# A decoder layer on one core: weight blocks rounded and subtracted whole, and the products of the feed-forward units accumulated in another order

## The chip, the cores and the metric

The kernel runs on one core of one Trainium2 chip. The metric is the device time of one execution in microseconds. The median of three executions of the kernel before is 1142.85 us (1142.00 to 1143.32).

## What is computed

One decoder layer on x of 512 tokens by 1024 features, all in float32: a feed-forward half-step, a mixer (attention in several forms), a second feed-forward half-step and a last norm.

```python
x = x + 0.5 * swiglu(rmsnorm(x, norm_ffn1), ffn1_w_in, ffn1_w_out)
x = x + hybrid_mixer(rmsnorm(x, norm_mix), ...)     # compressed, selected, windowed and dilated attention, gates
x = x + 0.5 * swiglu(rmsnorm(x, norm_ffn2), ffn2_w_in, ffn2_w_out)
return rmsnorm(x, norm_final)

def swiglu(h, w_in, w_out):            # w_in 1024 x 5632, w_out 2816 x 1024
    u, v = jnp.split(h @ w_in, 2, axis=-1)
    return (jax.nn.silu(u) * v) @ w_out
```

## The kernel before

**Three passes.** Each float32 product is made of three matmuls on rounded parts: hi x hi, hi x lo, lo x hi. ScalarE writes the rounded part of a weight block (`w_hi`, an ACTIVATE), VectorE subtracts it from the block (`w_lo`, a TENSOR_TENSOR), and TensorE needs both. Two slots of `w_hi` and `w_lo` alternate, so ScalarE can round the block of step g only when TensorE has finished step g - 2.

**The feed-forward block** is a list of segments (`SEGMENTS`): P (the narrow first block, features in 256 columns, straight products), U1, D0, U2, U3, D1, U4, U5, D2. A U segment makes 512 columns of both halves of w_in. It does this by a scheme of seven products of half-size blocks instead of eight: seven steps, each with its own combination of activation blocks (`A11`, the sums `S1` to `S4`, ...) and of weight blocks (`OPERAND`), and the results are combined into gate and value. One step is 2 x 12 matmuls of 128x512, first for token group g = 0, then g = 1. The weight combinations (`dve_diff`, `dve_t1`, `dve_t2`, `dve_t4`) are VectorE instructions of 128x2048 in the raw buffers. The gated products of one U unit are turned by TensorE (`pe_turn`, two halves) and split again into `pu_hi`, `pu_lo` (`act_turned`, `dve_turned`); the PSUM banks 6 and 7 hold both halves in turn, so half 1 is turned only after the `pu_lo` of half 0. A D segment multiplies two turned units with w_out, in four steps, and adds into `x_nat`. The whole block runs twice, i = 0 before the mixer and i = 1 behind it.

**Order.** Every engine's instructions are written out by hand in a fixed order; the semaphores in `up_sems` count what is done. For U units it stands in `act_unit`, `dve_unit` and `pe_unit`, for P in `act_plain`, `dve_plain`, `pe_plain`. `pe_bank_free` says which read of a bank TensorE waits for. In the attention part `pe_attend` goes by pairs of `ITEMS`: it transposes the probabilities of items n and n + 1, fills in a piece of projection (`pe_fill`), makes the scores of n + 2 and n + 3, then the value products of n and n + 1. Item 5 is the compressed attention; its scores are 128 very small matmuls (two records each in the trace).

**Head.** SyncE's queue brings four weight pairs of the P block (`load_pair`) and x (`load_x`) by turns, a weight pair first.

Of the kernel before, what the change touches and what calls it, by code (L numbers as in the profile page):

```python
# [26 lines left out]
ALU = mybir.AluOpType  # L27
# [7 lines left out]
P = 128  # L35
T = 512
# [65 lines left out]
def build(nc, x, positions, norm_ffn1, ffn1_w_in, ffn1_w_out, norm_mix, w_in, cmp_pos, cmp_w1, cmp_w2,  # L102
# [3 lines left out]
    with outer:  # L106
# [51 lines left out]
        A11, S3, A12, S1, S4, S2, A22 = range(7)  # L158
        SUMS = (S3, S1, S4, S2)
# [138 lines left out]
        B11, B12, B21, B22, B_DIFF, B_MINUS = range(6)  # L298

        def raw_of(u, b):  # L300
            return raws[{B11: 2, B12: 3, B22: 1, B21: 0, B_DIFF: 4, B_MINUS: 2}[b]]

        OPERAND = (B11, B_DIFF, B21, B12, B22, B_MINUS, B21)
        D_RAW = (3, 1, 2, 4)

        def op_raw(g):

            kind, n, g0 = [seg for seg in SEGMENTS if seg[2] <= g][-1]
            if kind == "P":
                return raws[4 - g]  # L310
            if kind == "U":
                return raw_of(n, OPERAND[g - g0])
            return raws[D_RAW[g - g0]][:, 0:ktiles_of(2 * n + (g - g0) % 2) * T]

        RAW_COUNT, raw_at = [0] * 5, {}
        for kind, n, g0 in SEGMENTS[1:]:
            for b, r in ((B11, 2), (B12, 3), (B22, 1), (B21, 0)) if kind == "U" else enumerate(D_RAW):
# [5 lines left out]
        for j in range(N_UNITS):  # L323
# [42 lines left out]
                   "plain": 1 + TT, "silu_plain": TT, "minus": 5, "diff": 5, "t1_ready": 5, "t2_ready": 5, "t4_ready": 5,  # L366
                   "op_hi": 2 * OPS, "op_lo": 2 * OPS, "product": 70, "down": 48, "chain_copied": 30, "v11": 10, "w7": 10,
                   "w5": 10, "e1": 10, "u12": 10, "y": 10, "v21": 10, "silu12": 10, "silu22": 10, "prod1": 12, "prod2": 12,
# [234 lines left out]
        def up_bank(kind, g, u):  # L603
            return ps[:, {"chain": 0, "first": 2, "second": 4}[kind] + g, 0:cols_of(u)]
# [28 lines left out]
        def op_landed(eng, i, g, half):  # L633
# [10 lines left out]
            elif o in (0, 2, 4):  # L644
                r, value = raw_at[kind, n, OPERAND[o]]
                eng.wait_ge(raw_landed[r], value + i * RAW_COUNT[r])
            else:
                eng.wait_ge(*up(i, {1: "diff", 3: "t1_ready", 5: "t2_ready", 6: "t4_ready"}[o], n))
# [45 lines left out]

        def load_up(sp, i, u, b, wi):
# [12 lines left out]
        def load_down(sp, i, d, o, wd):  # L708
# [3 lines left out]
            sp.dma_start(raws[D_RAW[o]][:, 0:nk * T].rearrange("p (k c) -> p k c", k=nk),  # L712
                         ktiles(wd[0])[:, k0:k0 + nk, half * T:half * T + T]).then_inc(raw_landed[D_RAW[o]], 16)

        def sync_up(sp, i, wi, wd):

            for kind, n, g in SEGMENTS[2:]:
                if kind == "D":
                    u, g0 = 2 * n + 1, first_op("U", 2 * n + 1)
                    sp.wait_ge(*up(i, "op_lo", 2 * (g0 + 4)))  # L720
                    load_down(sp, i, n, 0, wd)
                    sp.wait_ge(*up(i, "op_lo", 2 * (g0 + 5)))
                    load_down(sp, i, n, 1, wd)
                    sp.wait_ge(*up(i, "t2_ready", u))
                    load_down(sp, i, n, 3, wd)
                    sp.wait_ge(*up(i, "op_lo", 2 * (g0 + 6)))
                    sp.wait_ge(*up(i, "t4_ready", u))
                    load_down(sp, i, n, 2, wd)
                elif before_unit(n)[0] == "U":
                    g0 = first_op("U", n - 1)  # L730
                    sp.wait_ge(*up(i, "op_lo", 2 * (g0 + 4)))
                    load_up(sp, i, n, B12, wi)
                    sp.wait_ge(*up(i, "op_lo", 2 * (g0 + 5)))
                    load_up(sp, i, n, B22, wi)
                    sp.wait_ge(*up(i, "op_lo", 2 * (g0 + 6)))
                    sp.wait_ge(*up(i, "t4_ready", n - 1))
                    load_up(sp, i, n, B11, wi)
                    sp.wait_ge(*up(i, "op_lo", 2 * (g0 + 7)))
                    load_up(sp, i, n, B21, wi)
                else:  # L740
# [3 lines left out]
                    sp.wait_ge(*up(i, "op_lo", 2 * (gd + 1)))  # L744
                    load_up(sp, i, n, B12, wi)
                    sp.wait_ge(*up(i, "op_lo", 2 * (gd + 2)))
                    load_up(sp, i, n, B22, wi)
                    sp.wait_ge(*up(i, "op_lo", 2 * (gd + 3)))
                    load_up(sp, i, n, B11, wi)
# [9 lines left out]
        def _(sp):  # L759
            xv = x[0].rearrange("(t p) d -> p t d", p=P)  # L760

            def load_x(part, m0, m1, n):
                for tt in range(0, TT, n):
# [1626 lines left out]
```

## Time and profile before

| | |
|---|---|
| median of 3 runs | 1142.85 us |
| the profiled execution, its own time | 1144.03 us |
| its span, first to last instruction | 1142.2 us |
| TensorE busy | 1123.4 us, 98% |
| VectorE, ScalarE busy | 788.8 us, 517.7 us |

TensorE works nearly without a hole. Its matmuls overlap, so one of 128x512 has a duration of 0.39 us in the records but the next one starts 0.227 us later; a step of a U unit takes 24 of these, 5.44 us. In the timelines below a row gives the start, the time, the engine, the line, the operation and, in brackets, the idle time before it with what ended it.

### The profile page before, as it was taken

Reading aid. Unit: us, or ns where it says so; the run is one execution under the profiler, and the core shown is the slowest. Engines: PE = TensorE matmul, PEld = TensorE weight load, DVE = VectorE, ACT = ScalarE, POOL = GpSimd, SP = SyncE. Lnnn points to the kernel's source line nnn. Section 1 sums busy time; section 2 is a strip of 40 time slices with the busy share of each in tenths; the row PEclk is TensorE's granted clock in tenths of the full one; section 3 lists DMA queues with packets and bytes.
Section 4 is the critical chain, followed back from the end, with each engine's and each line's share of the span. In section 5 each row is a group of like instructions: output and inputs, shape, how many; then the busy total and the mean of one; then the engine's idle time right before and its main releaser. Section 6 shows DMA issues by size and latency. Waiting matters only on the chain.

```text
span 1142.2 us, 16722 instructions
## 1 busy us (share of the span) xinstructions
PE 1123.4 (98%) x6799; PEld 925.1 (81%) x6799; DVE 788.8 (69%) x1110; ACT 517.7 (45%) x757; POOL 137.0 (12%) x174
## 2 busy tenths in 40 slices
PE   8999999999999999999999999999999999999997
PEld 6778888888888987877778888888887888888885
DVE  7985888679955466566676344555795789459845
ACT  6642564245534233443445523356742565146533
POOL 1000000000010472346771000000000000000000
PEclk9999999999999999999999999999999999999999
DMA  8051326113514631413132232522052226204401
GB/s 305 24 203 37 111 74 221 37 43 106 184 47 122 153 84 43 96 54 82 45 83 50 75 101 80 181 90 101 10 184 74 74 74 221 74 8 141 147 1 74
DMA packets 111548, 111.78 MB, mean 98 GB/s; under 512 B 30896, under 2 KB 76384, under 8 KB 111472
## 3 DMA queue, kind: packets, MB, share of 16 engines
q1 hardware_dynamic: 106912, 104.97, 29.0%
q0 software_dynamic: 4400, 5.61, 1.8%
q8 instruction: 54, 0.88, 0.3%
q14 instruction: 22, 0.18, 0.1%
q10 hardware_dynamic: 160, 0.14, 0.0%
HBM read 105.71 MB, written 2.10 MB: 94 GB/s over the span
## 4 chain that ended last, share of the span: by engine, by line
PE 90%; DVE 7%; ACT 1%; issue 1%; DMA 0%; SPq 0%; DVEq 0%; ACTq 0%
PE ps L1994 11%; PE ps L1996 11%; PE ps L1995 11%; PE ps L1844 9%; PE ps L1845 8%; PE ps L1846 8%; PE ps L2010 6%; PE ps L2011 6%; PE ps L2012 6%; PE ps L1912 2%; PE ps L2128 2%; PE ps L2172 1%; PE ps L2201 1%; DVE w_lo L1500 1%; DVE probs L1458 1%
## 5 line engine op out<-in xcount | busy, mean ns | idle before, releaser
L1500 DVE TENSOR_TENSOR w_lo<-raw,w_hi 128x1024 fp32r<-128x1024 f32 (+1 forms) x124 | 142.0, 1185 | 65.0 <-ACT w_hi L1007 64.9
L1007 ACT ACTIVATE w_hi<-raw 128x1024 fp32r<-128x1024 f32 (+1 forms) x124 | 121.0, 1024 | 115.3 <-PE ps L2012 108.2
L2010 PE MATMUL ps<-w_hi,pu_hi 128*128 128x512 f32 x352 | 138.3, 393 | 0.1
L2012 PE MATMUL ps<-w_hi,pu_lo 128*128 128x512 f32 x352 | 137.1, 389 | 0.0
L2011 PE MATMUL ps<-w_lo,pu_hi 128*128 128x512 f32 x352 | 137.1, 389 | 0.0
L1994 PE MATMUL ps<-w_hi,xg_hi 128*128 128x512 f32 x320 | 125.3, 392 | 1.5 <-DVE square L1604 1.5
L1995 PE MATMUL ps<-w_lo,xg_hi 128*128 128x512 f32 x320 | 124.6, 389 | 0.0
L1996 PE MATMUL ps<-w_hi,xg_lo 128*128 128x512 f32 x320 | 124.5, 389 | 0.0
L1270 DVE TENSOR_TENSOR w_lo<-w_raw,w_hi 128x1024 fp32r<-128x1024 f32 (+4 forms) x42 | 75.3, 1793 | 54.6 <-ACT w_hi L890 54.6
L1844 PE MATMUL ps<-xg_hi,w_hi 128*128 128x512 f32 x272 | 108.5, 399 | 0.0
L1846 PE MATMUL ps<-xg_hi,w_lo 128*128 128x512 f32 x272 | 106.1, 390 | 0.0
L1845 PE MATMUL ps<-xg_lo,w_hi 128*128 128x512 f32 x272 | 106.0, 390 | 0.0
L1007 ACT ACTIVATE w_hi<-w_raw 128x1024 fp32r<-128x1024 f32 x72 | 72.2, 1052 | 66.3 <-PE ps L1996 66.3
L890 ACT ACTIVATE w_hi<-w_raw 128x2048 fp32r<-128x2048 f32 (+2 forms) x30 | 55.8, 1861 | 88.7 <-PE ps L1846 76.2
L1994 PE MATMUL ps<-w_hi,sum_hi 128*128 128x512 f32 x240 | 93.9, 391 | 0.0
L1996 PE MATMUL ps<-w_hi,sum_lo 128*128 128x512 f32 x240 | 93.4, 389 | 0.0
L1995 PE MATMUL ps<-w_lo,sum_hi 128*128 128x512 f32 x240 | 93.4, 389 | 0.0
L1500 DVE TENSOR_TENSOR w_lo<-w_raw,w_hi 128x1024 fp32r<-128x1024 f32 x72 | 84.6, 1216 | 5.0 <-ACT w_hi L1007 5.0
L2010 PEld LDWEIGHTS ps<-w_hi,pu_hi 128*128 128x128 f32 x352 | 66.1, 188 | 14.1 <-DVE pu_lo L1561 0.9
L2012 PEld LDWEIGHTS ps<-w_hi,pu_lo 128*128 128x128 f32 x352 | 66.1, 188 | 13.7
L2011 PEld LDWEIGHTS ps<-w_lo,pu_hi 128*128 128x128 f32 x352 | 66.1, 188 | 13.3
L1994 PEld LDWEIGHTS ps<-w_hi,xg_hi 128*128 128x128 f32 x320 | 60.1, 188 | 14.7 <-DVE square L1604 2.4
(287 smaller groups left out, 2155.9 us busy)
## 6 DMA issues: line engine op xcount, KB each, us to landing
raw<-in_ffn_w_in SPq DMA_DIRECT2D x20, 1024.0 KB, 4.9
w_raw<-in_ffn_w_in SPq DMA_DIRECT2D x20, 1024.0 KB, 5.0
w_raw<-in_w_in SPq DMA_DIRECT2D x32, 512.0 KB, 4.3
raw<-in_ffn_w_out SPq DMA_DIRECT2D x14, 1024.0 KB, 5.9
w_raw<-in_ffn_w_out SPq DMA_DIRECT2D x6, 1024.0 KB, 4.9
w_raw<-in_w_in SPq DMA_DIRECT2D x24, 256.0 KB, 3.9
raw<-in_ffn_w_in SPq DMA_DIRECT2D x16, 256.0 KB, 5.7
w_raw<-in_w_out SPq DMA_DIRECT2D x8, 512.0 KB, 4.4
```

Source lines behind the costliest of these rows:

```text
L1007: nc.scalar.activation(w_hi[:, (BASE[i] + g) % 2, part], op_raw(g)[:, part], ACT.Copy).then_inc(up_sems["op_hi"], 1)
L1270: lo = V.tensor_tensor(w_lo[:, s, c], w_raw[:, s, c], w_hi[:, s, c].bitcast(F32), ALU.subtract)
L1500: V.tensor_tensor(w_lo[:, sl, part], op_raw(g)[:, part], w_hi[:, sl, part].bitcast(F32), ALU.subtract).then_inc(up_sems["op_lo"], 1)
L1844: mm(out, ah, bh, start=(first and i == 0), stop=False)
L1845: mm(out, ah, bl, start=False, stop=False)
L1846: last = mm(out, al, bh, start=False, stop=(final and i == len(pairs) - 1))
L1994: mm(bank, ah, wh, start=(k == 0 and not goes_on), stop=False, skip_group_check=goes_on)
L1995: mm(bank, ah, wl, start=False, stop=False, skip_group_check=goes_on)
L1996: last = mm(bank, al, wh, start=False, stop=(k == 3), skip_group_check=goes_on)
L2010: mm(bank, ph, wh, start=(k == 0 and start), stop=False)
L2011: mm(bank, ph, wl, start=False, stop=False)
L2012: last = mm(bank, pl, wh, start=False, stop=(stop and k == nk - 1))
```

## The change

- `act_op` and `dve_op` round and subtract the weight block of every step from the third on (g >= 2) in one instruction of 128x2048 each; before, in two of 128x1024. TensorE's wait for the first half of a block is so a wait for all of it.
- The seven steps of a U unit come in another order, with three pairs of banks ("x", "z", "y"): steps 3, 4 and 5 go on accumulating in bank x on top of what is there, step 6 in bank y. VectorE's fourteen combinations of a unit become six (`dve_v11`, `dve_c22`, `dve_v21`), ScalarE's negated copy (`act_minus`) is gone. Step 5 now waits for `dve_c22`, which reads bank x after step 4.
- U1 has an order of its own (`dve_first_unit`); the P unit's two halves are turned after steps 1 and 3 of U1, before after steps 0 and 1.
- In the first P block, one sum, the difference for U1 and the copy of the other gains come later on VectorE.
- In the attention, the scores of item 5 are made in two portions around the value products of item 2, and the filled-in projection comes before the transposes of item 5.
- The first portion of x is loaded ahead of the first weight pair. The loads of later blocks follow the new release order of the raw buffers.

```diff
@@ OPERAND, raw buffers of the down steps
-        OPERAND = (B11, B_DIFF, B21, B12, B22, B_MINUS, B21)
-        D_RAW = (3, 1, 2, 4)
+        OPERAND = (B11, B_DIFF, B21, B_T2, B12, B22, B21)
+        D_RAW = ((4, 2, 3, 1), (4, 2, 3, 1), (4, 2, 3, 4))
@@ block.sync
+            load_x(sp, 0, 0, 2, 2)
             load_pair(sp, 0, 0, ffn1_w_in)
-            load_x(0, 0, 2, 2)
             load_pair(sp, 0, 1, ffn1_w_in)
@@ act_op (dve_op alike)
-            for half in range(2):
-                act_op_half(act, i, g, half)
+            if g < 2:
+                for half in range(2):
+                    act_op_half(act, i, g, half)
+                return
+            op_landed(act, i, g, 0)
+            op_slot_free(act, i, g)
+            w = op_raw(g).shape[1]
+            nc.scalar.activation(w_hi[:, (BASE[i] + g) % 2, 0:w], op_raw(g), ACT.Copy).then_inc(up_sems["op_hi"], 2)
@@ new: the combination that step 5 waits for
+        def dve_c22(dve, i, u, g):
+            n = u - 1
+            dve.wait_ge(*up(i, "product", 14 * n + 8 + g + 1))
+            dve.wait_ge(*up(i, "chain_copied", 6 * n + 2 + g + 1))
+            V.tensor_tensor(lane(u, g, 1), up_bank("x", g, u), lane(u, g, 1), ALU.add).then_inc(up_sems["c22"], 1)
@@ pe_bank_free
+            elif o == 5:
+                pe.wait_ge(*up(i, "c22", 2 * n + g + 1))
             else:
-                pe.wait_ge(*up(i, "v11", 2 * n + g + 1))
+                pe.wait_ge(*up(i, "chain_copied", 6 * n + {3: 0, 4: 4, 6: 2}[o] + g + 1))
@@ dve_plain
             if i == 0:
                 dve_rstd(dve, 0)
-                dve_more_gains(dve)
-            dve_diff(dve, i, 1)
+                dve_sum(dve, i, S4)
+            else:
+                dve_diff(dve, i, 1)
...
+                if i == 0 and tt == 1:
+                    dve_diff(dve, i, 1)
@@ pe_unit
-                if u % 2 and o < 2:
+                if u > 1 and u % 2 and o < 2:
                     pe_turn(pe, i, u - 1, o)
+                elif u == 1 and o in (1, 3):
+                    pe_turn(pe, i, 0, o // 2)
@@ pe_attend
                 pe_transpose_probs(pe, n)
+                first = n + 1 < b and ITEMS[n + 1][0] == "cmp"
+                if first:
+                    pe_fill(pe, n)
                 if n + 1 < b:
                     pe_transpose_probs(pe, n + 1)
...
                 for nn in (n, n + 1):
                     if nn < b - 1:
                         pe_values(pe, nn)
+                    if nn == n and n + 3 < b and ITEMS[n + 3][0] == "cmp":
+                        pe_scores(pe, n + 3, 1)
```

VectorE in U1 of the second feed-forward block (i = 1), from the two scalings of the P unit on. Before, where `pu_lo` is the split of the turned P unit, `raw<-raw,raw` a weight combination and `w_lo<-w_raw` the subtraction of a step:

```order
L1604 SCALAR_TENSOR_TENSOR scratch<-ps,rstd_col,scratch 128x256 [waits up_silu_plain] x2
L1500 TENSOR_TENSOR w_lo<-raw_87,w_hi 128x1024 [waits up_op_hi] x2
L1524 TENSOR_TENSOR raw_86<-raw_86,raw_85 128x2048 [waits up_diff,up_minus]
L1500 TENSOR_TENSOR w_lo<-w_raw,w_hi 128x1024 [waits up_op_hi] x2
L1561 TENSOR_TENSOR pu_lo_82<-ps,pu_hi_80 128x2x128 [waits up_p_hi] x2
L1500 TENSOR_TENSOR w_lo<-raw_86,w_hi 128x1024 [waits up_op_hi] x2
L1529 TENSOR_TENSOR raw_85<-raw_85,raw_87 128x2048 [waits up_t1_ready]
```

and now, the same stretch:

```order
L1641 SCALAR_TENSOR_TENSOR scratch<-ps,rstd_col,scratch 128x256 [waits up_silu_plain] x2
L1524 TENSOR_TENSOR w_lo<-raw_87,w_hi 128x2048 [waits up_op_hi]
L1524 TENSOR_TENSOR w_lo<-w_raw,w_hi 128x2048 [waits up_op_hi]
L1544 TENSOR_TENSOR raw_85<-raw_87,raw_85 128x2048 [waits up_op_lo,up_diff]
L1524 TENSOR_TENSOR w_lo<-raw_85,w_hi 128x2048 [waits up_op_hi]
L1549 TENSOR_TENSOR raw_86<-raw_85,w_raw 128x2048 [waits up_t2_ready]
L1524 TENSOR_TENSOR w_lo<-raw_86,w_hi 128x2048 [waits up_op_hi]
L1598 TENSOR_TENSOR pu_lo_82<-ps,pu_hi_80 128x2x128 [waits up_p_hi] x2
L1524 TENSOR_TENSOR w_lo<-w_raw,w_hi 128x2048 [waits up_op_hi]
L1571 TENSOR_TENSOR tmp_b<-ps,tmp_b 128x512 [waits up_chain_copied,up_product]
L1598 TENSOR_TENSOR pu_lo_82<-ps,pu_hi_80 128x2x128 [waits up_p_hi] x2
L1556 TENSOR_TENSOR w_raw<-w_raw,raw_85 128x2048 [waits up_op_lo,up_t1_ready,up_t2_ready]
```

The split of the first turned half moved from behind the subtraction of step 2 to behind that of step 4; each combination now reads the one before it, and the last one (`w_raw<-w_raw,raw_85`, the block of step 6) stands behind the subtraction of step 5. After it come the second `dve_c22` (L1571 on `scratch`), two `dve_v11` and the subtraction of step 6.

VectorE in U2, from its third combination on, where the L1571 rows are `dve_c22`. Now:

```order
L1524 TENSOR_TENSOR w_lo<-raw_86,w_hi 128x2048 [waits up_op_hi]
L1556 TENSOR_TENSOR w_raw<-w_raw,raw_85 128x2048 [waits up_op_lo,up_t1_ready,up_t2_ready]
L1524 TENSOR_TENSOR w_lo<-w_raw,w_hi 128x2048 [waits up_op_hi]
L1571 TENSOR_TENSOR tmp_b<-ps,tmp_b 128x512 [waits up_chain_copied,up_product]
L1571 TENSOR_TENSOR scratch<-ps,scratch 128x512 [waits up_chain_copied,up_product]
```

Here the two `dve_c22` stand behind the whole subtraction of step 5 itself; before, nothing of VectorE behind that subtraction was awaited by step 5.

TensorE around the scores of item 5, where `k_cmp` marks them, `probs` the transposes and `v_nsa` the value products (the fills of 24 matmuls in between are left out). Before:

```order
L2114 MATMUL ps<-k_cmp,pool 32x32 x128
L2201 MATMUL ps<-probs_t,v_nsa 64x128 x12
...
L2172 MATMUL ps<-const,probs 128x128 x8
L2159 MATMUL ps<-const,probs 128x128 x8
...
L2128 MATMUL ps<-pool 32x512 x8
```

and now:

```order
L2168 MATMUL ps<-k_cmp,pool 32x32 x64
L2256 MATMUL ps<-probs_t,v_nsa 64x128 x6
L2168 MATMUL ps<-k_cmp,pool 32x32 x64
L2256 MATMUL ps<-probs_t,v_nsa 64x128 x6
...
L2227 MATMUL ps<-const,probs 128x128 x8
...
L2214 MATMUL ps<-const,probs 128x128 x8
L2183 MATMUL ps<-pool 32x512 x8
```

A fill stands now between the transposes of item 4 (L2227) and of item 5 (L2214).

## Rows read from the trace of the kernel before

**Rows 1.** The page, busy time of TensorE's matmuls.
```profile
PE 1123.4 (98%) x6799; PEld 925.1 (81%) x6799; DVE 788.8 (69%) x1110; ACT 517.7 (45%) x757; POOL 137.0 (12%) x174
```
**Rows 2.** What TensorE waited for: us in total, times, longest.
```profile
PE ps L2114 <- issue: 2.4, 1, 2.4
PE ps L2159 <- DVE probs L1446: 1.9, 1, 1.9
...
PE ps L1912 <- DVE pu_lo L1561: 1.3, 2, 0.6
```
**Rows 3.** Timeline of the first feed-forward block, from P to U1.
```profile
32.39 0.39 PE L1964 MATMUL ps<-w_hi,xg_lo 128*128 128x512 f32 x1
...
32.91 2.28 DVE L1518 TENSOR_TENSOR raw<-raw,w_raw 128x2048 f32<-128x2048 f32 x1
33.50 0.47 ACT L1086 ACTIVATE scratch<-ps,rstd_col 128x256 f32<-128x256 f32 x1
35.10 0.87 DVE L1604 SCALAR_TENSOR_TENSOR square<-ps,rstd_col,square 128x256 f32<-128x256 f32 x2
35.64 0.50 PE L1994 MATMUL ps<-w_hi,xg_hi 128*128 128x512 f32 x1 [1.50 <-DVE square L1604]
```
**Rows 4.** Groups by form: busy us, mean ns of one.
```profile
L1500 DVE TENSOR_TENSOR w_lo<-raw,w_hi 128x1024 fp32r<-128x1024 f32 x116 | 136.8, 1219 | 63.4 <-ACT w_hi L1007 63.4
L1518 DVE TENSOR_TENSOR raw<-raw,w_raw 128x2048 f32<-128x2048 f32 x10 | 22.9, 2286 | 0.4
L1635 DVE TENSOR_TENSOR square<-ps,tmp_a 128x512 f32<-128x512 f32 x10 | 6.8, 679 | 0.0
L1561 DVE TENSOR_TENSOR pu_lo<-ps,pu_hi 128x256 fp32r<-128x256 f32 x8 | 3.0, 414 | 0.0
L890 ACT ACTIVATE w_hi<-w_raw 128x2048 fp32r<-128x2048 f32 x25 | 47.8, 1914 | 81.0 <-PE ps L1846 73.9 <-PE ps L2012 7.1
```
**Rows 5.** Timeline of U2, around its steps 4 and 5.
```profile
133.45 2.00 ACT L1007 ACTIVATE w_hi<-raw 128x1024 fp32r<-128x1024 f32 x2
...
138.19 0.39 PE L1994 MATMUL ps<-w_hi,sum_hi 128*128 128x512 f32 x1
```
**Rows 6.** Timeline at the start of D0.
```profile
75.48 2.01 ACT L1007 ACTIVATE w_hi<-w_raw 128x1024 fp32r<-128x1024 f32 x2 [2.54 <-PE ps L1996]
...
80.18 1.28 DVE L1561 TENSOR_TENSOR pu_lo<-ps,pu_hi 128x512 fp32r<-128x512 f32 x2
...
81.01 0.63 PE L1912 MATMUL ps<-const,tmp_b 128*128 128x128 f32 x4 [0.65 <-DVE pu_lo L1561]
```
**Rows 7.** Timeline of the second feed-forward block, P and U1.
```profile
802.98 2.00 ACT L1007 ACTIVATE w_hi<-raw 128x1024 fp32r<-128x1024 f32 x2
...
812.74 0.50 PE L1994 MATMUL ps<-w_hi,xg_hi 128*128 128x512 f32 x1
...
819.01 2.00 ACT L1007 ACTIVATE w_hi<-w_raw 128x1024 fp32r<-128x1024 f32 x2
```
**Rows 8.** Timeline of the head.
```profile
4.85 1.06 ACT L1007 ACTIVATE w_hi<-raw 128x1024 fp32r<-128x1024 f32 x1 [1.58 <-DMA raw<-in_ffn_w_in]
...
7.47 1.10 PE L1890 MATMUL ps<-const,x_nat 128*128 128x128 f32 x8 [1.08 <-DMA x_nat<-in_x]
...
8.97 0.50 PE L1968 MATMUL ps<-w_hi,xg_hi 128*128 128x512 f32 x1 [0.41 <-ACT xg_hi L895]
```
**Rows 9.** Timeline of TensorE at items 4 and 5.
```profile
455.51 1.04 PE L2172 MATMUL ps<-const,probs 128*128 128x128 f32 x8
458.45 1.16 PE L2159 MATMUL ps<-const,probs 128*128 128x128 f32 x8 [1.90 <-DVE probs L1446]
...
463.84 1.79 PE L2128 MATMUL ps<-pool 64*32 64x512 f32 x48
```
**Rows 10.** Windows: length, busy, granted clock, DMA share, GB/s.
```profile
460.00:461.00 1.00, 1.00 (x7) 0.50 0.19 64
```
**Rows 11.** The page, loads: count, KB each, us to landing.
```profile
raw<-in_ffn_w_in SPq DMA_DIRECT2D x20, 1024.0 KB, 4.9
```

More of the change, by code:

```diff
@@ L603, in up_bank @@
         def up_bank(kind, g, u):
-            return ps[:, {"chain": 0, "first": 2, "second": 4}[kind] + g, 0:cols_of(u)]
+            return ps[:, {"x": 0, "z": 2, "y": 4}[kind] + g, 0:cols_of(u)]
         def prod_lane(u, half, g):
@@ L1096, in act_unit @@
             act_op(act, i, g0 + 2)
-            if prev is not None:
+            if u > 1 and prev is not None:
                 for g in range(2):
@@ L1102, in act_unit @@
             act_op(act, i, g0 + 3)
-            if prev is not None:
+            if u > 1 and prev is not None:
                 for g in range(2):
@@ L1503, in dve_op @@
         def dve_op(dve, i, g):
-            for half in range(2):
-                dve_op_half(dve, i, g, half)
+            if g < 2:
+                for half in range(2):
+                    dve_op_half(dve, i, g, half)
+                return
+            sl, w = (BASE[i] + g) % 2, op_raw(g).shape[1]
+            dve.wait_ge(*up(i, "op_hi", 2 * g + 2))
+            V.tensor_tensor(w_lo[:, sl, 0:w], op_raw(g), w_hi[:, sl, 0:w].bitcast(F32),
+                            ALU.subtract).then_inc(up_sems["op_lo"], 2)
         def dve_diff(dve, i, u):
@@ L1586, in dve_plain @@
                 dve_op(dve, i, 1)
-            for o in (S1, S2, S4):
+            for o in (S1, S2, S4) if i else (S1, S2):
                 dve_sum(dve, i, o)
@@ L1613, in dve_unit @@
                 dve_v21(dve, i, prev, 1)
+            if u == 1:
+                dve_first_unit(dve, i, g0)
+                return
             dve_op(dve, i, g0 + 1)
-            if u == 1 and i == 0:
-                for o in SUMS[1:]:
-                    dve_sum_lo(dve, i, o)
             if prev:
@@ L1653, in dve_unit, with dve_first_unit @@
                 dve_diff(dve, i, u + 1)
[L1654 to L1660 removed]
+                dve_op(dve, i, g0 + 7)
             dve_prod1(dve, i, u, 0)
             dve_prod1(dve, i, u, 1)
+            if u % 2:
+                dve_op(dve, i, g0 + 7)
+        def dve_first_unit(dve, i, g0):
+            dve_op(dve, i, g0 + 1)
+            if i == 0:
+                dve_sum_lo(dve, i, S2)
+            dve_op(dve, i, g0 + 2)
+            dve_t2(dve, i, 1)
+            if i == 0:
+                dve_sum_lo(dve, i, S1)
+            dve_op(dve, i, g0 + 3)
+            dve_t1(dve, i, 1)
+            if i == 0:
+                dve_sum_lo(dve, i, S4)
+            dve_op(dve, i, g0 + 4)
+            for g in range(2):
+                dve_turned(dve, i, 0, 0, g)
+            dve_op(dve, i, g0 + 5)
+            dve_c22(dve, i, 1, 0)
+            for g in range(2):
+                dve_turned(dve, i, 0, 1, g)
+            dve_t4(dve, i, 1)
+            dve_c22(dve, i, 1, 1)
+            for g in range(2):
+                dve_v11(dve, i, 1, g)
+            dve_op(dve, i, g0 + 6)
+            dve_prod1(dve, i, 1, 0)
+            dve_prod1(dve, i, 1, 1)
+            dve_op(dve, i, g0 + 7)
         def dve_add(dve, i, d, half, tt):
@@ L1986, in pe_unit @@
                     pe_bank_free(pe, i, u, o, g)
-                    bank = up_bank("first" if o in (2, 6) else "second" if o == 4 else "chain", g, u)
+                    bank = up_bank("z" if o == 2 else "y" if o in (1, 6) else "x", g, u)
                     for k in range(4):
@@ L2107, in pe_scores @@
                        start=True, stop=False)
-                for qt in range(TT):
+                for qt in range(2 * part, 2 * part + 2):
                     for hh in range(HPG):
@@ L2230, in pe_attend @@
                 pe_transpose_probs(pe, n)
+                first = n + 1 < b and ITEMS[n + 1][0] == "cmp"
+                if first:
+                    pe_fill(pe, n)
                 if n + 1 < b:
                     pe_transpose_probs(pe, n + 1)
-                if n in FILL:
+                if n in FILL and not first:
                     pe_fill(pe, n)
```

213 lines of the change are left out of this document (104 added, 109 removed).

## The prediction

> **What bounds the kernel now.** I read the page first: TensorE's matmuls are busy 98% of the span [rows 1], so the sum over instructions of the other engines says nothing; only what opens or closes a hole in TensorE's row of work counts. The view of TensorE's waits comes next. It lists the holes: one of 2.4 us at the small score matmuls that no engine released, one of 1.9 us before the transposes of item 5 and two of 0.6 us at the starts of D0 [rows 2], and one of 1.5 us at the start of U1 in the first block [rows 3]. That is 7.1 us in all, and there is no idle wait inside U2 to U5, which says that VectorE and ScalarE keep ahead there. So the change has little to win, and the reader should see in the timelines how far ahead the two engines are at each step. After a hole the first matmul needs 0.1 us more (0.50 against 0.39 us [rows 3]).
>
> **Whole instead of halves.** One subtraction of 128x1024 takes 1.22 us, one VectorE instruction of 128x2048 in SBUF 2.29 us, one rounding of 128x2048 1.91 us [rows 4]; the next VectorE instruction starts 2.2 us after such a one (32.91 to 35.10 [rows 3]). By halves, VectorE can begin when ScalarE has half the block: two roundings take 2.0 us together [rows 5], so it begins 1.1 us after ScalarE and what is queued behind the subtraction starts 1.1 + 2.3 = 3.4 us after. Whole, it is 1.95 + 2.2 = 4.15 us. So all that hangs on the subtraction is 0.75 us later, while both engines save under 0.1 us a block. Where TensorE has slack this is hidden by its 5.44 us step.
>
> The Trainium skill speaks for the whole form in one place and against it in another. "VectorE: DVE Perf Modes", in its section on the TRN2 errata, says that a large tile pays the fixed latency once and small ones each time; the rows agree in size (2.29 against 2 x 1.22 us). "Perfetto Trace Analysis", in its section on optimizing Scalar and DVE operations, says that where these engines are not saturated but cause bubbles elsewhere, breaking up instructions may let work be completed sooner. By the first rule alone the whole form costs nothing and the sum below would lose all its terms but those of the head, the reorderings and the attention; by the second it is the sum below.
>
> VectorE has 30% of the span free [rows 1], and TensorE already waits behind a subtraction at D0 [rows 2]; so I count the delay, not the saving, where a wait of TensorE hangs on a subtraction.
>
> **U2 to U5, eight units.** Step 5 now waits for the first `dve_c22`, which is queued behind the whole subtraction of step 5. In U2 ScalarE starts that rounding at 133.45 [rows 5] (the bank copy ahead of it is unchanged), so the subtraction starts at 135.40, `dve_c22` at 137.60 and, with 0.68 us [rows 4], ends at 138.28; 0.1 us later TensorE can go. Step 5 starts at 138.19 today [rows 5]. That is 0.2 us late, 0.3 with the slow first matmul. The eight `tensor_tensor` and the negated copy that a unit loses lay beside the matmuls and are worth nothing. Eight units: +2.4 us. From both sides: nothing if the three durations are together 0.2 us shorter, +4.0 if they are 0.2 us longer. The other blocks have 0.5 us and more to spare by the same sum (odd units, step 3: rounding at S2 + 0.6, ready at + 4.85, needed at + 5.4).
>
> **D0, twice.** The turn of half 1 waits for the `pu_lo` of half 0, and this stands behind the subtraction of D0's second block and two products. ScalarE starts at 75.48, the first `pu_lo` at 80.18, TensorE goes at 81.01 after a wait of 0.65 us [rows 6]. All of it moves by the 0.75 us. Nothing covers it, TensorE already waits. Twice: +1.5 us. The bounds are 0 and +2.
>
> **U1 of the second block.** Four places, all from the orders shown.
> - The P unit's scaling frees the bank for step 0 and stands behind the whole subtraction of that step. Rounding starts at 802.98; TensorE goes at 812.74 [rows 7], hard behind VectorE. Whole: rounded at 804.88, subtraction from 804.92, its successor from 807.12 against 806.6 in the run before: +0.5 us. Start of U1 813.27; step 1 at 818.8 (5.44 + 0.1).
> - From the rounding of step 2 a chain runs without slack, each link needing the last: round and subtract step 2, combination T2, round and subtract step 3, combination T1, round and subtract step 4, first `pu_lo`. The rounding of step 2 follows the end of step 0 and starts 6.27 us after U1, as before (812.74 to 819.01 [rows 7]), at 819.5. Three times 1.95 + 2.2, two combinations of 2.3 and 0.4 for `pu_lo` [rows 4] are 17.5 us: 837.0. TensorE reaches the turn of half 1 after steps 1, 2 and 3 and one turn at 818.8 + 16.4 + 0.5 = 835.7. Late by 1.3 us, with the restart 1.4.
> - The second `dve_c22` stands behind the combination for step 6: step 5 starts at 843.2, its g = 1 half is due at 845.9, but VectorE has the subtraction until 842.2, `dve_c22` 0.6, two splits 0.7, the combination 2.2 and `dve_c22` 0.7, that is 846.4: +0.6 us.
> - Step 6's block is rounded only after that combination (845.8): 1.95 + 2.2 + 0.1 give 850.1, TensorE is there at 849.3: +0.8 us.
> Together with restarts +3.75 us for U1 and, as above, its D0. Bounds: +1.5 (if only the start and the turn cost) and +5.
>
> **U1 of the first block.** The difference for U1 (2.28 us from 32.91) no longer stands ahead of the scalings, so the hole of 1.5 us before 35.64 goes [rows 3]: U1 starts at 34.0, -1.66 us. But the difference now follows the second scaling: that tile's last matmul starts at 32.39, its silu needs 0.47 and its scaling 0.44 [rows 3], so it is about 33.8; difference until 36.05, rounding until 38.0, subtraction until 40.3. Step 1 is due at 34.0 + 5.44 = 39.4: a new hole of 1.0 us. Behind it the same three places as above cost 0.4 (the chain starts at 40.1 there and TensorE is later), 0.65 and 0.85 us. Net +1.2 us, between -1.5 and +3.
>
> **The head.** Weights land first, rounding starts at 4.85; x lands at 7.45, its transposes start at 7.47, TensorE's first real matmul at 8.97 [rows 8]. The queue serves in order and both portions have the same size, so I swap the two landings: weights at 7.45, rounding to 8.5, subtraction (1.2 us) to 9.75, first matmul at 9.87. x is ready earlier to no use: +0.9 us. Bounds: -1.0 (if both land by 5) and +2.5.
>
> **The attention.** The chain from the scores of item 5 to its probabilities is VectorE's and stays. The fill (24 matmuls, 2.95 us) now covers the wait of 1.9 us before 458.45 [rows 9]. After that wait the granted clock stood at 0.50 [rows 10], that is 1.2 GHz, and the fill ran at half pace; without the hole I expect 2.4 GHz, which gives back 1.5 us. From 455.51 to 463.84 [rows 9] are 8.33 us; without the two it is 1.0 + 2.95 + 0.95 = 4.9, so -3.4 us. The hole of 2.4 us without a releaser [rows 2] comes after 192 records of tiny matmuls; if it is a matter of supplying instructions, it ends when it ends and the value products moved before it (0.7 us) are hidden in it: -0.7. The scores of item 7 now wait some 0.3 us for a copy: in all -3.8 us. Bounds: -6 (the 2.4 us go too) and -1.
>
> **Sum.** 2.4 + 1.5 + 3.75 + 1.2 + 0.9 - 3.8 = +5.95 us against the profiled execution: span 1142.2 to 1148.2, its own time 1144.03 to about 1150.0. The profiled run lay 1.2 us over the median; on the median of 1142.85 it gives 1148.8 us.
>
> **Rivals.**
> A. *No step is late* (about 1141.5 us, faster). If VectorE and ScalarE, with some 50 us less of combinations, run ahead enough that step 5 and the U1 chain are in time, then only the removed holes remain: -1.5 at U1, -3.8 in the attention, +0.9 at the head, +1.5 at D0, +1.5 left in U1: -1.4. For it speaks that VectorE was nearly full in U3 and U5; against it, that each late chain above begins with a rounding that waits for TensorE's slot, which no free time moves forward. It decides if the time from that rounding to the end of `dve_c22` is under 4.65 us; I have 4.83.
> B. *The new waits are as computed, but the attention pays more* (about 1145 us): all of the 2.4 us goes and `dve_c22` costs nothing. Between the forecast and no change.
> C. *The head's hole drops the clock* (about 1150.5 us). TensorE would idle 2.5 us before 9.87 after little work, and after the waits in the attention the records show half pace [rows 10]; about 1.5 us more. The Trainium skill's page "TensorE: Matmul & The Clock Gate", section on the clock gate, says that an idle array falls back to 1.2 GHz and must work again for full rate; against it stands that 2.4 us without work at the small scores was followed by rows at full clock.
> D. *B22 lands late.* The block B22 is loaded one step later than today, and the difference for the odd unit waits for it with a subtraction behind it. A load of 1 MB lands 4.9 us after its issue [rows 11]. Issued when step 5's block is subtracted (137.7 in U2), it is there at 142.6 to 143.9, the latter if two loads ahead of it hold the queue; the difference and the subtraction of the next unit's first block end then by 148.3, and that unit starts at 149.1. If loads took 2 us longer in four places: +5 us, 1154.
>
> **Chances.** The forecast with its terms about as above 0.55, C 0.10, D 0.07 (all slower), B 0.12, A 0.16. A measurement can tell 0.2%, 2.3 us, from no change. Slower by over 0.2%: 0.55 + 0.10 + 0.07 and a third of B, 0.76. Within: the rest of B and a quarter of A, 0.12. Faster: 0.12. The range goes from 1142.5, which leaves out A, to 1153.
>
> **What would show it.** Waits of TensorE on `dve_c22` (L1571), about 0.2 us in each of eight units, and longer ones in both U1; the waits on `pu_lo` at D0 grown from 0.65 to 1.4 us and new ones at the turn in U1; the wait at step 1 of the first U1 on the subtraction; first real matmul near 9.9 us; no wait before the transposes of item 5 and clock 1.00 behind it. The forecast is wrong if TensorE's idle total does not rise, or if step 5 of U2 starts without a wait.

## The result and the profile after

| | before | after |
|---|---|---|
| median | 1142.85 us (5 runs, 1141.64 to 1143.72) | 1153.74 us (5 runs, 1152.96 to 1155.58) |
| profiled execution, own time / span | 1144.03 / 1142.2 us | 1153.42 / 1151.6 us |

The ratio is 1.0102, 95% interval 1.009 to 1.0114: slower by 10.9 us. Forecast were 1148.8 us and a range up to 1153.0. The sign was right, the size was not: the sum said +5.95 us, the two profiled executions differ by +9.4, the medians by +10.9. Two executions at a far lower mean clock, one of e8 (1887.54 us at 0.556) and one of the kernel before (1405.33 us at 0.751), are left out of all ratios below.

The page of the kernel after, against [rows 1] and [rows 11]: VectorE lost 50 us of work and 174 instructions, TensorE's busy time grew by 4.4 us, and the large loads land later.

```profile
PE 1127.8 (98%) x6799; PEld 922.8 (80%) x6799; DVE 738.7 (64%) x936; ACT 491.8 (43%) x653; POOL 136.7 (12%) x174
...
raw<-in_ffn_w_in SPq DMA_DIRECT2D x20, 1024.0 KB, 5.3
w_raw<-in_ffn_w_in SPq DMA_DIRECT2D x20, 1024.0 KB, 5.9
```

TensorE's waits of the kernel after (total, times, longest), against [rows 2]. L1964 is a turn, L2046 a step of a U unit, L2020 the P block, L2168 the scores of item 5.

```profile
PE ps L1964 <- DVE pu_lo L1598: 4.8, 4, 1.5
PE ps L2046 <- DVE w_lo L1524: 3.6, 5, 1.0
...
PE ps L2020 <- DVE w_lo L1513: 1.3, 1, 1.3
PE ps L2168 <- issue: 1.2, 1, 1.2
PE ps L2046 <- DVE scratch L1571: 0.9, 2, 0.5
PE ps L2046 <- DVE square L1641: 0.7, 1, 0.7
```

Where the feed-forward blocks had 1.3 us of waits on splits (at D0) and one of 1.5 us on a scaling (at U1 [rows 3]), there are now 4.8 us on splits, 3.6 us on subtractions, 0.9 us on `dve_c22` and 0.7 us on a scaling. The wait of 1.9 us before item 5 is gone.

**By place.** Of both profiled executions I took the time at which TensorE starts each segment. A segment's length is the distance from its start to the next one's, and the table gives by how much the change made it longer:

| place | forecast | seen |
|---|---|---|
| head, to the first real matmul (8.97 to 9.54) | +0.9 | +0.57 |
| first block, P and U1 | +1.2 | +1.9 |
| D0, first and second block | +1.5 | +1.75 |
| first block, U2 to U5 | +1.2 | +2.8 |
| attention and mixer | -3.8 | -4.26 |
| second block, start of U1 and U1 | +3.75 | +4.57 |
| second block, U2 to U5 | +1.2 | +1.45 |
| last down steps to the end | 0 | +0.64 |
| sum | +5.95 | +9.4 |

D0 in the kernel after, against [rows 6]; first VectorE, then TensorE:

```profile
79.98 2.29 DVE L1524 TENSOR_TENSOR w_lo<-raw,w_hi 128x2048 fp32r<-128x2048 f32 x1 [1.41 <-ACT w_hi L1019]
82.19 0.74 DVE L1584 SCALAR_TENSOR_TENSOR tmp_b<-square,rstd_col,tmp_b 128x512 f32<-128x512 f32 x1
82.85 0.74 DVE L1584 SCALAR_TENSOR_TENSOR scratch<-scratch,rstd_col 128x512 f32<-128x512 f32 x1
83.51 1.28 DVE L1598 TENSOR_TENSOR pu_lo<-ps,pu_hi 128x512 fp32r<-128x512 f32 x2
```
```profile
84.34 0.63 PE L1964 MATMUL ps<-const,tmp_b 128*128 128x128 f32 x4 [1.50 <-DVE pu_lo L1598]
```

ScalarE rounds from 77.96 to 79.9 in one piece, so VectorE idles 1.41 us, subtracts, makes two products and only then splits. TensorE waits 1.50 us against 0.65.

U1 of the second block in the kernel after, VectorE, against [rows 7]:

```profile
836.71 2.29 DVE L1524 TENSOR_TENSOR w_lo<-raw,w_hi 128x2048 fp32r<-128x2048 f32 x1 [2.10 <-ACT w_hi L1019]
838.92 0.75 DVE L1598 TENSOR_TENSOR pu_lo<-ps,pu_hi 128x256 fp32r<-128x256 f32 x2
842.55 2.29 DVE L1524 TENSOR_TENSOR w_lo<-w_raw,w_hi 128x2048 fp32r<-128x2048 f32 x1 [2.88 <-ACT w_hi L1019]
...
846.02 2.28 DVE L1556 TENSOR_TENSOR w_raw<-w_raw,raw 128x2048 f32<-128x2048 f32 x1
848.22 0.69 DVE L1571 TENSOR_TENSOR scratch<-ps,scratch 128x512 f32<-128x512 f32 x1
```

Look at the idle times in brackets, 2 to 3 us on the engine that TensorE waits for: each `w_lo` waits for a whole rounding, which waits for a combination made by this same engine. The first `pu_lo` ends after 839.3, and TensorE turned at 839.48 after a wait of 1.21 us.

The start of U3 in the kernel after, VectorE and then TensorE; before, TensorE did not wait there:

```profile
149.04 2.29 DVE L1538 TENSOR_TENSOR raw<-raw,w_raw 128x2048 f32<-128x2048 f32 x1 [2.39 <-DMA w_raw<-in_ffn_w_in]
151.25 2.28 DVE L1524 TENSOR_TENSOR w_lo<-raw,w_hi 128x2048 fp32r<-128x2048 f32 x1
```
```profile
153.68 0.47 PE L2046 MATMUL ps<-w_hi,xg_hi 128*128 128x512 f32 x1 [0.76 <-DVE w_lo L1524]
```

The difference waits for the block B22, and the first block of U3 is subtracted behind it. Counted from the start of U2, B22 was issued at 20.7 us before and at 26.8 us now, and took 6.44 us to land before and 7.85 us now (issued at 141.11, landed at 148.96). The two loads ahead of it were issued at 137.51 and 137.93 us.

### The profile page after: what moved, and what is told of

Same layout as the page of the kernel before. It is cut to its first block, busy times and chain, and to the rows that moved or that the text cites. A ratio compares the mean times of both kernels' runs of the same rounds, so it can differ in the third digit from the quotient of the medians.

```text
span 1151.6 us, 16477 instructions
## 1 busy us (share of the span) xinstructions
PE 1127.8 (98%) x6799; PEld 922.8 (80%) x6799; DVE 738.7 (64%) x936; ACT 491.8 (43%) x653; POOL 136.7 (12%) x174
## 4 chain that ended last, share of the span: by engine, by line
PE 81%; DVE 8%; ACT 5%; issue 4%; DMA 1%; SPq 0%; DVEq 0%; ACTq 0%
PE ps L1896 9%; PE ps L1898 8%; PE ps L1897 8%; PE ps L2046 8%; PE ps L2048 8%; PE ps L2047 8%; PE ps L2064 6%; PE ps L2066 6%; PE ps L2065 6%; ACT w_hi L1019 4%; DVE w_lo L1524 2%; PE ps L1964 2%; PE ps L2183 2%; PE ps L2227 1%; PE ps L2256 1%
## 5 line engine op out<-in xcount | busy, mean ns | idle before, releaser
L1524 DVE TENSOR_TENSOR w_lo<-raw,w_hi 128x2048 fp32r<-128x2048 f32 (+1 forms) x60 | 133.2, 2220 | 71.4 <-ACT w_hi L1019 71.4
L1019 ACT ACTIVATE w_hi<-raw 128x2048 fp32r<-128x2048 f32 (+1 forms) x60 | 111.5, 1858 | 154.2 <-PE ps L2066 80.3
L2064 PE MATMUL ps<-w_hi,pu_hi 128*128 128x512 f32 x352 | 138.5, 393 | 0.0
L2046 PE MATMUL ps<-w_hi,xg_hi 128*128 128x512 f32 x320 | 127.0, 397 | 4.5 <-DVE w_lo L1524 2.5
L1524 DVE TENSOR_TENSOR w_lo<-w_raw,w_hi 128x2048 fp32r<-128x2048 f32 x34 | 77.9, 2292 | 50.1 <-ACT w_hi L1019 49.9
L2046 PE MATMUL ps<-w_hi,sum_hi 128*128 128x512 f32 x240 | 94.2, 393 | 1.2 <-DVE w_lo L1524 1.2
L1019 ACT ACTIVATE w_hi<-w_raw 128x2048 fp32r<-128x2048 f32 x34 | 64.8, 1907 | 33.6 <-PE ps L2066 29.3
L2046 PEld LDWEIGHTS ps<-w_hi,xg_hi 128*128 128x128 f32 x320 | 60.1, 188 | 23.1 <-issue 4.6
```

The costliest lines, as they stand in the source:

```text
L1019: nc.scalar.activation(w_hi[:, (BASE[i] + g) % 2, 0:w], op_raw(g), ACT.Copy).then_inc(up_sems["op_hi"], 2)
L1524: V.tensor_tensor(w_lo[:, sl, 0:w], op_raw(g), w_hi[:, sl, 0:w].bitcast(F32), ALU.subtract).then_inc(up_sems["op_lo"], 2)
L2046: mm(bank, ah, wh, start=(k == 0 and not goes_on), stop=False, skip_group_check=goes_on)
L2064: mm(bank, ph, wh, start=(k == 0 and start), stop=False)
```

## The experiments

Each ran on the same chip as runs of the kernel before, against which its ratio stands. The kernel before took 1142.16 us beside e1 to e4, 1142.40 beside e5 to e8 and 1142.84 beside e9 to e12, so differences to the 1153.74 us of the kernel after hold to some 0.7 us.

**e1_orders_halves.** All orders of the change, the halves back:

```diff
-            if g < 2:
...
-            w = op_raw(g).shape[1]
-            nc.scalar.activation(w_hi[:, (BASE[i] + g) % 2, 0:w], op_raw(g), ACT.Copy).then_inc(up_sems["op_hi"], 2)
+            for half in range(2):
+                act_op_half(act, i, g, half)        # dve_op alike
```

> The changed kernel with every block again rounded and subtracted in two halves; all its orders stay. Theory 1 (the whole form costs latency wherever TensorE waits behind a subtraction, and the orders themselves cost little): the eight waits of 0.2 us at step 5 go, the wait on pu_lo at D0 falls from 1.5 to about 0.7 us, the three holes in each U1 after its step 1 (2.3 and 3.0 us together) nearly go, the hole at step 1 of the first U1 falls from 1.1 to about 0.4 us, and the last down steps give back 0.65 us. That is some 10 us: about 1143, and with the scatter 1140 to 1144.5 us. Theory 2 (the new order of the products and the late loads cost by themselves): most holes stay and the time is 1150 us or more. The wait of VectorE for the block B22 ahead of U3 stays in both theories (about 1 us).

Measured: 1139.29 us, ratio 0.9975 (0.9965 to 0.9986), 14.4 us less than the kernel after. Theory 1 holds in kind, but the time lies 0.7 us below its range: its gain was put 3.7 us too small, in part because the start of U3 came back too (U2 and U3 take 78.02 us, 79.70 after, 77.95 before) and the hole of 1.1 us at step 1 of U1 went altogether. TensorE's waits in it:

```profile
PE ps L2008 <- DVE w_lo L1507: 2.6, 1, 2.6
...
PE ps L2156 <- issue: 1.4, 1, 1.4
PE ps L1952 <- DVE pu_lo L1586: 1.3, 2, 0.6
```

In the feed-forward blocks only the two waits at D0 are left, as long as before. The first row is the head.

**e2_whole_alone.** The kernel before with the whole form alone.

> The kernel before with the whole form alone; all orders as before. Theory 1 (latency): D0 twice 0.9 us, the start of U1 twice 0.6 us, the last down steps 0.65 us, no step waits for a combination behind a subtraction inside U2 to U5: +3.7 us, 1146.5 us (1144.5 to 1149). Theory 2 (the longer instructions cost in every step, also where there was slack): +8 us or more, over 1150 us. Theory 3 (fewer instructions pay): at or under 1142.8 us.

Measured: 1162.94 us, ratio 1.0182 (1.0168 to 1.0196), +20.8 us. Theory 1 fell in the size and theory 2 describes it better, though not "in every step": the waits stand at particular steps.

```profile
PE ps L2006 <- DVE w_lo L1516: 10.6, 10, 1.4
PE ps L1924 <- DVE pu_lo L1573: 3.6, 3, 1.5
```

Each odd unit waits 1.37 us at its start and 1.0 us at its step 4; a pair of units takes 81.5 to 81.8 us instead of 77.95. In the old order fourteen combinations fill VectorE around these places (before, it is busy without a gap from 138.5 to 156 us), so it seems that a rounding of 1.9 us that can't be overlapped is added to the chain; no run takes this apart. The new order and the other edits do help the whole form: 14.4 us of loss instead of 20.8. With halves U2 to U5 have no wait of TensorE to speak of in either order (77.95 and 78.02 us for U2 and U3).

**e3_attention_alone** and **e12_fill_alone.** The kernel before with the new order around item 5; e12 leaves its scores in one piece.

```diff
+                first = n + 1 < b and ITEMS[n + 1][0] == "cmp"
+                if first:
+                    pe_fill(pe, n)
...
-                if n in FILL:
+                if n in FILL and not first:
                     pe_fill(pe, n)
```

> The kernel before with the new order of scores, fill and transposes around item 5 alone. Theory 1: this is what gave the 4.3 us seen between the two traces in the attention, independent of the feed-forward blocks: about 1138.6 us (1137.8 to 1139.5). The hole before the transposes of item 5 is gone and the granted clock behind it is 1.00. Theory 2 (part of the 4.3 us came from elsewhere, such as a state of buffers or clock that the feed-forward block left): 1140 us or more.

> The kernel before with the fill moved ahead of the transposes of item 5, and the scores of item 5 in one piece as before. The two edits together measured 1139.7 us against 1142.2. Theory 1 (the fill covers the 1.9 us in which TensorE waited for VectorE, the split of the scores hides 0.7 us of value products in the hole that no engine released): fill alone about 1140.4 us, with a hole of 2.4 us among the small score matmuls as before. Theory 2 (all of the gain comes from the fill): 1139.7 us. Theory 3 (the hole among the scores sets the rest): 1141.5 us or more.

Measured: e3 1139.74 us, ratio 0.9982 (0.9973 to 0.999); e12 1140.37 us, ratio 0.9981 (0.9972 to 0.999), with the kernel before at 1142.84 in its company. So the two edits bring 2.4 us by the medians, not 4.3, and the fill alone brings as much. The mixer takes 475.78 us with the fill alone and 475.80 with both, 2.1 us less than before; both traces have a stretch at clock 0.50 behind the hole among the small scores. As bare times e3 lies between its two theories, and e12 is at the number of its theory 1. But the kernel before took 1142.84 us beside e12 and 1142.16 beside e3, so ratios and traces speak for theory 2 in both; the intervals, about 1 us to each side, could not tell 0.7 us apart. Between the traces, the rest of the 4.3 us is clock: with both edits and the clock at 1.00 the mixer takes 473.6 to 473.9 us in six of them (after, e1, e5, e9, e10, e11) and 474.4 us in e6. Windows of e3 and, below, of e1, behind the hole among the small scores (length, busy times, then the granted clock before the DMA share):

```profile
451.00:452.00 1.00, 1.00 (x34) 0.94 (x21) 0.72 (x1) 0.00 (x0) 0.00 (x0) 0.50 0.06 16
452.00:453.00 1.00, 1.00 (x9) 0.67 (x6) 0.93 (x3) 0.00 (x0) 0.00 (x0) 0.50 0.00 0
```
```profile
451.00:452.00 1.00, 1.00 (x9) 1.00 (x10) 0.93 (x3) 0.00 (x0) 0.00 (x0) 1.00 0.00 0
```

**e4_weights_first.** The changed kernel with the first weight pair ahead of x.

> The changed kernel with the first weight pair again ahead of the first portion of x on SyncE's queue. Theory 1 (the head's 0.57 us comes from the order of these two loads, since the first matmul waits for the subtraction of the weights): first real matmul back from 9.54 to about 8.97 us, time about 1153.2 us, 0.6 us less than the changed kernel. Theory 2 (what starts earlier at the head is lost again at the hole at step 1 of U1, which waits for VectorE and ScalarE): no change within 0.3 us.

Measured: 1153.73 us (4 runs), no difference to 1153.74. In its trace the first real matmul starts at 8.74 us and D0 0.83 us earlier, so the head and what hangs on it go as theory 1 says; nothing of it is lost again at step 1 of U1. Its profiled execution lost 1.5 us in the mixer, where the clock stood at 0.50 from 458 to 460 us. The medians can't tell the two orders apart; the trace can.

**e5_u1_order.** In U1, the split of the first turned half ahead of step 4 (on ScalarE too, which is left out here), the combination for step 6 between the subtractions of steps 4 and 5, and both `dve_c22` ahead of the split of the second turned half.

```diff
-            dve_op(dve, i, g0 + 4)
             for g in range(2):
                 dve_turned(dve, i, 0, 0, g)
+            dve_op(dve, i, g0 + 4)
+            dve_t4(dve, i, 1)
             dve_op(dve, i, g0 + 5)
             dve_c22(dve, i, 1, 0)
+            dve_c22(dve, i, 1, 1)
             for g in range(2):
                 dve_turned(dve, i, 0, 1, g)
-            dve_t4(dve, i, 1)
-            dve_c22(dve, i, 1, 1)
```

> The changed kernel, whole form kept, with another order in U1 on VectorE and ScalarE alone: the split of the first turned half stands ahead of the rounding and subtraction of step 4, the combination for step 6 stands between the subtractions of steps 4 and 5, and the split of the second turned half behind both dve_c22. Theory 1 (the holes in U1 come from what stands ahead of pu_lo, of the second dve_c22 and of the rounding of step 6 on these two engines): the six holes of 0.7, 0.6, 1.0 us in the first block and 1.4, 0.6, 1.0 us in the second go, each U1 keeps the 0.2 us at step 5 that the other units have; -4.7 us, about 1149 us. Theory 2 (the chain of roundings, subtractions and combinations is too long whatever stands between): the holes move to step 4 or 5 and the time falls by less than 2 us, 1152 us or more.

Measured: 1150.92 us (1149.15 to 1153.35), -2.8 us. Between the theories: in the second block the three holes of 3.0 us became one of 0.6, in the first block those of 2.3 us became one of 1.7 at step 4. That one is theory 2's:

```profile
53.88 1.22 DVE L1617 TENSOR_TENSOR xg_lo<-xs,xg_hi 128x1024 fp32r<-128x1024 f32 x1
55.60 0.76 DVE L1598 TENSOR_TENSOR pu_lo<-ps,pu_hi 128x256 fp32r<-128x256 f32 x2 [0.51 <-ACT pu_hi L1040]
57.76 2.29 DVE L1524 TENSOR_TENSOR w_lo<-raw,w_hi 128x2048 fp32r<-128x2048 f32 x1 [1.39 <-ACT w_hi L1019]
```

The chain up to step 4 is itself too long by whole blocks.

**e6_diff_late.** The difference for the odd unit behind the subtraction of its first block.

> The changed kernel, whole form kept, with the difference for the next odd unit behind the subtraction of that unit's first block instead of ahead of it. Theory 1 (the hole of 0.9 us at the start of U3 comes from the block B22, which VectorE waits 2.4 us for with that subtraction queued behind; rival D of the prediction): the waits of TensorE at the starts of U3 and U5 (0.9 and 0.3 us in the first block) go and the difference is still in time for step 1: -1.2 us, about 1152.5 us. Theory 2 (the difference is then late for step 1, as the load is late for both): the hole moves from step 0 to step 1, the same time or more.

Measured: 1157.39 us (1157.0 to 1160.17), 3.7 us more. It costs more, as theory 2 allowed, but not where either theory put it. TensorE's waits at the starts of U3 and U5 are gone, as theory 1 said, but there is none at step 1; the difference comes later (152.12 us instead of 149.04 in the first pair), ScalarE's rounding of step 1 waits for it, and the row of work behind it reaches the turns late: a new wait on `pu_lo` of 0.62 us in each of the four odd units. ScalarE in e6 and, below, in the kernel after:

```profile
154.49 1.93 ACT L1019 ACTIVATE w_hi<-raw 128x2048 fp32r<-128x2048 f32 x1 [4.11 <-DVE raw L1538]
```
```profile
153.04 1.92 ACT L1019 ACTIVATE w_hi<-raw 128x2048 fp32r<-128x2048 f32 x1 [2.95 <-PE ps L2048]
```

**e7_gated_first.** `dve_prod2` ahead of the subtraction in D.

```diff
-            dve_op(dve, i, g0 + 1)
             for g in range(2):
                 dve_prod2(dve, i, u, g)
+            dve_op(dve, i, g0 + 1)
```

> The changed kernel, whole form kept, with the two gated products (dve_prod2) ahead of the subtraction of a D segment's second block instead of behind it. VectorE idles 1.4 us there in D0, ahead of the subtraction, and the two products take 1.4 us. Theory 1 (pu_lo at D0 is late because of all that stands ahead of it on VectorE): the wait of TensorE at D0 falls from 1.5 us to about 0.2 us in both blocks; -2.6 us, about 1151.1 us. Theory 2 (the subtraction, pushed back by the products, makes the second step of D0 late): no gain.

Measured: 1152.00 us (1150.83 to 1154.2), -1.7 us. The waits at D0 fell from 1.50 and 1.52 to 0.21 and 0.54 us: theory 1, a little short. Its profiled execution, the slowest of the four, started 0.9 us late at the head (10.41), after a wait of 2.34 us, and the granted clock stood at 0.50 behind it:

```profile
11.00:12.00 1.00, 1.00 (x4) 0.81 (x3) 1.00 (x2) 0.04 (x1) 0.00 (x0) 0.50 1.06 387
12.00:13.00 1.00, 1.00 (x4) 0.81 (x3) 1.00 (x3) 0.00 (x0) 0.00 (x0) 0.50 1.04 394
```

The P block so took 26.42 us instead of the 24.99 of the kernel after.

**e10_round_whole** and **e11_subtract_whole.** The changed kernel with one engine whole and the other by halves.

> The changed kernel with ScalarE's rounding whole and VectorE's subtraction again in two halves. Theory 1 (the whole rounding makes VectorE start 0.9 us later, the whole subtraction makes TensorE wait for the second half as well): TensorE may start when the first half is subtracted, 1.1 us earlier, so the waits on w_lo (4.7 us with their restarts) and the 0.65 us of the last down steps go, while the waits on pu_lo at D0 and in U1 and on dve_c22 stay, some of them longer by what TensorE gained ahead: 1149 to 1151.5 us. Theory 2 (the whole rounding alone makes the loss): 1153 us or more. Theory 3 (the whole subtraction alone makes it): 1141 us or less.

> The changed kernel with ScalarE's rounding again in two halves and VectorE's subtraction whole, which has to wait for both halves. Theory 1: VectorE starts 0.1 us later than in the changed kernel (two roundings take 2.0 us, one 1.9), everything else stays: 1154 to 1155 us. Theory 2 (the whole rounding makes the loss by something else than its latency): 1145 us or less.

Measured: e10 1151.57 us (1149.66 to 1153.64), e11 1156.51 us (1154.37 to 1158.67). In e10 TensorE's waits on `w_lo` are gone from the units and those on `pu_lo` have grown, from 4.8 to 6.3 us; the end behind the last down steps stayed as long as after (53.95 us from the start of D2, 53.94 after), which theory 1 had wrong:

```profile
PE ps L1958 <- DVE pu_lo L1592: 6.3, 4, 1.7
...
PE ps L2040 <- DVE scratch L1565: 0.9, 2, 0.5
```

Theory 1 in kind, at the edge of its range. In e11 the waits at D0 and at step 5 are 0.1 us longer than after (step 5 starts 0.30 us late instead of 0.21, D0 waits 1.60), theory 1 in kind, but the median lies 1.5 us above its range. In its trace the head was late by 0.7 us besides, and the clock behind it 0.50 again, so that the P block took 26.57 us. So one whole instruction is enough for most of the loss, on whichever of the two engines: of the 14.4 us over e1, by the medians, 12.3 are there with the rounding alone whole and all (17.2) with the subtraction alone whole. What is lost is the overlap of the two, half against half, and it needs both by halves.

**e8_all_halves** and **e9_best.** e1 with the order of e5, the products of e7 and the first pair of e4; e8 has the late difference of e6 too.

> All in one, on the orders of the change with the halves back (measured 1139.3 us): the order in U1, the late difference, the gated products ahead at D, and the first weight pair ahead of x at the head. Expected by theory 1: the two waits of 0.63 us at D0 go with their restarts (-1.5 us) and the head gives 0.8 us; the other two edits give nothing where the halves already removed the holes: about 1137.0 us (1136.3 to 1138.5). By theory 2 (what is left is not set by these places): 1139 us.

> The run with everything in one, but the difference for the odd units back at its place ahead of the subtraction. Theory 1 (a late difference makes ScalarE's rounding of the odd units' step 1 late, which moved the pair U2, U3 from 78.02 to 78.21 us in each of four places): -0.8 to -1.0 us against the 1138.4 us measured with it: about 1137.5 us (1136.5 to 1138.2). Theory 2 (0.2 us a pair is within what scatters): no difference, 1138.4 us.

Measured: e8 1138.4 us, ratio 0.9958 (0.9945 to 0.997), at the upper edge of its theory 1. e9 1136.85 us (1136.55 to 1137.14), ratio 0.9946 (0.9932 to 0.996). e9 is the fastest kernel here, 6.0 us under the kernel before measured beside it and 16.9 under the changed one. Its median is in the range of its theory 1, and the traces agree: the four pairs of units together take 0.9 us less than in e8, as theory 1 said; the intervals of the two medians overlap. What is left of TensorE's waits in it:

```profile
PE ps L2309 <- DVE tmp_b L1797: 1.5, 1, 1.5
PE ps L2156 <- issue: 1.2, 1, 1.2
PE ps L2008 <- DVE w_lo L1507: 0.5, 1, 0.5
```

L2309 is the first matmul of all, ahead of the head.

## Why the prediction was right in sign and wrong in size

The trace holds 3.5 us more than the sum. Terms that were sized too small make 4.2 us: U2 to U5 of the first block (1.6), the two U1 (0.8 and 0.7), the last down steps, which the sum put at nothing (0.6), D0 and U2 to U5 of the second block (0.25 each). The attention and the head give 0.8 us back.

- **Whole costs latency (the 0.75 us): right, and the main cause.** e1 shows that the whole form alone carries 14.4 us, the other edits together are worth -2.9. The term came out at D0 (+0.89 and +0.85 for 0.75 each) and at step 5 of eight units (0.21 for 0.2, 0.35 with the slow first matmuls for 0.3). The Trainium skill's page "Perfetto Trace Analysis", section on optimizing Scalar and DVE operations, says that broken-up instructions may let work be completed sooner; this case agrees by 14.4 us, while VectorE was busy 744.3 us by halves (e1) against 738.7. The saving that "VectorE: DVE Perf Modes" of the Trainium skill, section on the TRN2 errata, promises for large tiles is there too and is those 5.6 us on VectorE; TensorE, busy 98% of the span, never sees them.
- **U2 to U5 of the first block: the step that failed most (+1.2 forecast, +2.8 seen).** I gave rival D, B22 landing late, 7 in 100, and took the loads' 4.9 us from [rows 11], a median, as they were, with up to 6.2 us where loads ahead hold the queue. B22 was issued at the step I had said, but took 7.85 us: the load issued 0.42 us behind another one took 7.49 us, and B22 came 3.2 us behind that. VectorE waited 2.4 us for B22 and TensorE 0.76 us at U3. So D came true in its mechanism, loads some 2 us longer, and not in its price: 1.0 and 0.3 us in two of four pairs, not 5 us; but it belonged into the sum. In e1 the same load took 7.81 us, and U2 and U3 took 78.02 us against 77.95, so the late load costs only together with the whole form of the subtraction behind it.
- **U1: kinds right, size too small (+1.2 and +3.75 forecast, +1.9 and +4.57 seen).** Seen in the second block, above the 0.2 us that a change of segment takes anyway: 0.6 at the start (0.5 forecast), 1.37 at the turn (1.4), 0.59 at `dve_c22` (0.6), 1.02 at step 6 (0.8), and 0.37 at step 3, which I had not. The five make 3.95; the other 0.6 us is the first matmuls behind each wait, about 0.12 us a wait. The four terms of the prediction make 3.3 us, and its restarts bring them to 3.75, so the restarts were nearly right, and the step that failed here is step 3, which it put at nothing, and step 6.
- **The last down steps: omitted (+0.64).** `dve_op` also serves D2. The first addition of the end stands behind its last subtraction, at 1125.75 us instead of 1116.12: 9.63 us late, where the matmuls were 8.76 late. From there VectorE and ScalarE carry the end, so the delay stays. e1 gave all of it back (53.30 us from the start of D2 to the end, 53.94 after).
- **Attention: -3.8 forecast, -4.26 seen, and -2.4 on medians.** The hole before item 5 is gone and the clock behind it is 1.00, as forecast. I took the whole gain of the clock off the median, though the profiled run of before lay 1.2 us over its median. Here lie the 1.5 us between +9.4 and +10.9: 1.2 us by which the profiled run of before was above its median, 0.3 by which that of after was below. What makes the 1.2 us stays open. The slow clock of [rows 10] alone does not: the mean clock of that run was 0.997, and 42 of the 43 executions of the kernel before beside the experiments have 0.997 or less as well. Where the slow stretch falls may decide: e2, with the attention of the kernel before, has it from 459.0 us on, ahead of the wait before item 5; that wait is then 0.87 us instead of 1.90 and the mixer takes 476.69 us instead of 477.94. That the median execution of before looks like this is not shown. The 0.7 us for the value products in the hole are not there on their own (e12).
- **Head: +0.9 forecast, +0.57 seen**, 0.8 in the pair of traces of e4. In seven traces with x first it was +0.1 to +1.4 us, so the near hit is in part luck.
- Rival A (no step is late) fell, and B did not matter. C (the head drops the clock) did not come in the trace of the kernel after, but it did in those of e7 and e11, whose first real matmul started at 10.41 and 10.20 us after waits of 2.34 and 2.05 us: the clock was 0.50 from 10.1 and 10.3 us to about 13.6, which cost 1.4 and 1.6 us in the P block; 1.5 us were forecast. A wait of 2.64 us in e1 (first matmul at 9.82) was followed by 1.00. Whether the slower executions of the kernel after had it is not known.

## What to carry over

Where one engine rounds and the next subtracts, the size of the pieces sets when the second can start; merging pieces saves little busy time and adds most of a piece of latency at each place where the third engine waits; here it was enough that one of the two engines was whole. Before pricing an edit to a helper, list every place that calls it, the tail too. Before crediting a gain that a profiled execution shows in its clock, ask whether the median has that loss, and where.

## What the runs showed that I had not expected

- The clock after nearly the same hole at the small scores differs from run to run: 1.43 us of idleness were followed by 0.50 in e3 (450.8 to about 454 us) and by 1.00 in e1. Of e3's eleven runs six lie between 1139.54 and 1139.74 us, five between 1140.56 and 1141.94; the profiled one, with the slow clock, is the slowest. The slow clock can't be all of the difference: of the five, three have a mean clock of 0.996 or 0.997, but two have 0.998 and 0.999, as the six have.
- That hole is 2.1 to 2.4 us with the scores in one piece (before, e2, e12) and 1.1 to 1.5 us in ten of eleven kernels with them in two (1.8 in e6), without the mixer being shorter for it: 475.78 us in e12, 475.80 in e3. It came after 192 small records in all three of the one kind and after 180 in all eleven of the other, and no engine released it. What ends it stays open.
- With x first, the first real matmul started anywhere from 9.05 to 10.41 us in seven executions (after, e1, e5, e6, e7, e10, e11); with the weights first from 8.39 to 9.04 in seven (before, e2, e3, e4, e8, e9, e12). So the head scatters more with x first; what sets its place in that spread stays open.
